# A sliding-window attention layer inside a 17-phase kernel: the attention of the first key heads is issued among the query projections

## The chip, the cores and the metric

The kernel runs on one core of a Trainium2 chip. The metric is device microseconds for one execution, the median of several. Before the change three runs gave 2635.97 us (2631.42 to 2639.07). Engines: PE (TensorE) with its weight loads PEld, DVE (VectorE), ACT (ScalarE), POOL (GpSimd) and SP (SyncE), which here only issues DMAs. The sequence is 256 tokens, the width 1024.

## The reference

Four layers of a mixed network, then a second block. Each layer is feed-forward, mixer, feed-forward, gated projection. The mixer of the third layer (index 2) is the sliding-window attention, and only that one is touched:

```python
def swa_mixer(x, w_qkv, q_gain, k_gain, sinks, w_o):
    q, k, v = jnp.split(x @ w_qkv, [nq, nq + nk], axis=-1)      # 16 query heads, 4 key heads of 64
    q = rmsnorm(q.reshape(B, T, SW_HEADS, SW_HD), q_gain)
    k = rmsnorm(k.reshape(B, T, SW_KV_HEADS, SW_HD), k_gain)
    ...
    s = jnp.einsum('bnqkgd,bnskd->bnkgqs', qb, kk).astype(jnp.float32) * (SW_HD ** -0.5)
    s = s - slopes[:, :, None, None] * dist
    s = jnp.where(valid[None, :, None, None], s, -jnp.inf)      # window of 128 keys
    probs = jax.nn.softmax(jnp.concatenate([s, sink], axis=-1), axis=-1)[..., :-1]
    o = jnp.einsum('bnkgqs,bnskd->bnqkgd', probs.astype(vv.dtype), vv).reshape(B, T, nq)
    return o @ w_o
```

## The kernel before

All weights are cut into units of 128 x 2048 floats (1 MB, 256 output columns over all 1024 inputs). SP loads each unit into one of four raw buffers (L586 in the loop). ACT rounds it to the high part (`high`, L1129), DVE subtracts that from the raw unit to get the low part (`low`, L1535), and PE multiplies high by high, low by high and high by low. Three units have room in split form: `high(m)` waits until unit m-3 has been used, `low(m)` waits for `high(m)`, and PE waits for `low(m)`. Here `n0` is the first unit of the phase, and `low(n0 + u + SPLIT)` prepares the unit three places on.

`project` (L658) runs one unit as 48 matmuls of 256 columns into one PSUM bank; `project_tokens` (L675) does the same with tokens in the rows. Banks 0 to 3 form a ring; DVE empties a bank by `scale` (L1594) or `scale_tokens` (L1600), multiplying by the root of the layer's norm, and counts it in `bank_read`.

The sliding-window phase `sw` has 11 units: in order two of keys, four of queries, one of values, four of the output matrix. Each unit of keys or queries is a pair of 128-feature chunks. Each pair has its own norm per head: ACT squares it (L1412), PE sums the squares by a matmul with a block matrix (`sums`, L1012), ACT takes Ln (L1400) and then Exp (L1406) of the sums, DVE multiplies the pair (`normalise`, L2078). Ln and Exp each come behind a load of the activation table. Before, pairs 0 to 3 do this together and pairs 4 and 5 together.

Then comes the attention, 8 groups: group g is key head g // 2 and query block g % 2, with four query heads. An even group sees 128 keys, an odd one 256. Steps of a group: `scores` (PE, L969), `logits` (DVE: bias L2109, maximum L2036, small sinks L2040 to L2042), `exps` (ACT, L1371 and L1375), `probs` (DVE, L2050 to L2054), `turn` (PE transposes, L979), `copies` (ACT, L1390), `values` (PE, L989), `take` (DVE, L2060). All score banks are double (banks 0 to 3), and so are the value banks (6 and 7); `scores(g + 2)` is issued ahead of `turn(g)`, and `values(g - 1)` behind it. Last, ACT and DVE split the result into two parts (L1423, L2116) and the four output units run (`w_out`), the first of them waiting for each part as it needs it.

Each engine runs its own program in strict order; the order is written out by hand in the function `sw` of each engine, and semaphores join them.

Of the kernel before, what the change touches and what calls it, by code (L numbers as in the profile page):

```python
# [14 lines left out]
P = 128  # L15
# [72 lines left out]
def weight_units(inputs, phases):  # L88
# [3 lines left out]
    for kind, layer in phases:  # L92
# [29 lines left out]
        elif kind == "sw":  # L122
            w = a["sw_w_qkv"][0]
            for u in range(2):
                k0 = SW_HEADS * HD + 2 * u * HD
                yield columns_unit(w, np.concatenate([span(k0, HD), span(k0, HD), span(k0 + HD, HD), span(k0 + HD, HD)]))
# [172 lines left out]
def build(nc, phases, x_t, p_t, mem_t, weights, smalls_d, post_rows, c_common, c_levels, c_swa, c_second, out):  # L299
    begin = starts(phases)  # L300
    NU = begin[-1]["units"]
    with ExitStack() as ctx:
# [173 lines left out]
        def sw_pair(u):  # L476

            c = 8 + 2 * u if u < 2 else 2 * (u - 2)
            return SW_QK[:, c:c + 2]

# [155 lines left out]
        def _(pe):  # L636
# [318 lines left out]
            def attention(g0, groups, bufs, read="exp", late=False):  # L955
# [4 lines left out]
                def scores(g):  # L960
                    if g >= len(groups):
                        return
                    if g >= 2:
                        pe.wait_ge(att[read], g0 + g - 1)
# [18 lines left out]
                def values(g):  # L983
                    pe.wait_ge(att["pt"], g0 + g + 1)
                    if g >= 2:
                        pe.wait_ge(att["taken"], g0 + g - 1)
                    for r, col, vs in groups[g]["values"]:
                        for j, (v, block_) in enumerate(vs):
                            last = nc.tensor.matmul(ps[r, 6 + g % 2, col:col + P], v,  # L989
                                                    PT[g % 2][:, block_ * P:(block_ + 1) * P],  # L990
                                                    start=(j == 0), stop=(j == len(vs) - 1))
# [12 lines left out]
                values(len(groups) - 1)  # L1004

            def sw(i):
# [114 lines left out]
        def _(act):  # L1121
# [237 lines left out]
            def attention(g0, groups, bufs, sinks=False, from_psum=False):  # L1359
                PR, PT = bufs  # L1360

                def exps(g):
                    if g == len(groups):
                        return
# [3 lines left out]
                    if from_psum and g >= len(PR):  # L1368
                        act.wait_ge(att["turned"], g0 + g - len(PR) + 1)
                    if sinks:  # L1370
                        nc.scalar.activation(t[:, 12:16], t[:, 12:16], ACT.Exp, scale=G["scale"])  # L1371
                    for s in range(G["slots"]):
                        p = PR[g % len(PR)][:, s * G["width"] + G["k0"]:(s + 1) * G["width"]]
                        src = ps[:, 2 * (g % 2) + s // 2, (s % 2) * 256:(s % 2 + 1) * 256] if from_psum else p
                        last = nc.scalar.activation(p, src, ACT.Exp, bias=t[:, 4 + s:5 + s], scale=G["scale"],  # L1375
# [3 lines left out]
                exps(0)  # L1379
                for g, G in enumerate(groups):  # L1380
                    exps(g + 1)
# [8 lines left out]
                    nc.scalar.copy(dst, src).then_inc(att["pt"], 1)  # L1390

            def sw(i):
# [3 lines left out]

                def roots(p0, p1):
                    for p in range(p0, p1):
                        act.wait_ge(m["sums"], p + 1)
                        ins = nc.scalar.activation(  # L1400
                            SW_SQ[:, 2 * (p % 4):2 * (p % 4) + 2].rearrange("p c t -> p (c t)"), ps[:, 4 + p % 4, :],
                            ACT.Ln, bias=EPSB, scale=1.0 / HD)
                    link(ins)
                    for p in range(p0, p1):
                        r = SW_SQ[:, 2 * (p % 4):2 * (p % 4) + 2]
# [915 lines left out]
```

## Time and profile before

| what | value |
|---|---|
| median of three runs | 2635.97 us |
| the profiled execution, its own time | 2631.93 us |
| its span | 2630.1 us |
| mean granted clock of TensorE | 0.994 |
| PE busy | 2564.0 us (97%) |
| DVE busy | 1729.3 us (66%) |
| ACT busy | 1203.6 us (46%) |
| mean DMA traffic | 167 GB/s |

The profiled execution took 1.8 us outside its span. All times below are microseconds from the start of the span. Busy time counts an engine as busy while an instruction is in flight, and matmuls overlap each other, so the distance from start to start is the cost of one.

### The profile page before, as it was taken

Reading aid. Unit: us, or ns where it says so; the run is one execution under the profiler, and the core shown is the slowest. Engines: PE = TensorE matmul, PEld = TensorE weight load, DVE = VectorE, ACT = ScalarE, POOL = GpSimd, SP = SyncE. Lnnn points to the kernel's source line nnn. Section 1 sums busy time; section 2 is a strip of 40 time slices with the busy share of each in tenths; the row PEclk is TensorE's granted clock in tenths of the full one; section 3 lists DMA queues with packets and bytes.
Section 4 is the critical chain, followed back from the end, with each engine's and each line's share of the span. In section 5 each row is a group of like instructions: output and inputs, shape, how many; then the busy total and the mean of one; then the engine's idle time right before and its main releaser. Section 6 shows DMA issues by size and latency. Waiting matters only on the chain.

```text
span 2630.1 us, 49686 instructions
## 1 busy us (share of the span) xinstructions
PE 2564.0 (97%) x21160; PEld 2522.5 (96%) x21160; DVE 1729.3 (66%) x2225; ACT 1203.6 (46%) x1277; POOL 29.4 (1%) x62
## 2 busy tenths in 40 slices
PE   8999999999999999999988999999999999999998
PEld 8999999999998999999977999999999999999998
DVE  6557666576566765765576656755866657688664
ACT  4435254444444544453464434534535435444643
POOL 0000000000000000000000000000000000011000
PEclk9999999999999999999999999999999999999999
DMA  6454235544543454454532445544424554445352
GB/s 270 181 187 173 99 134 195 189 176 178 183 170 143 149 192 180 178 184 178 188 134 78 184 176 176 188 181 177 175 97 159 198 177 175 169 133 168 142 188 76
DMA packets 62130, 439.19 MB, mean 167 GB/s; under 512 B 7504, under 2 KB 7632, under 8 KB 9488
## 3 DMA queue, kind: packets, MB, share of 16 engines
q1 hardware_dynamic: 59440, 429.05, 44.8%
q0 software_dynamic: 2528, 7.74, 1.1%
q8 instruction: 131, 2.15, 0.3%
q14 instruction: 31, 0.25, 0.0%
HBM read 432.56 MB, written 1.05 MB: 165 GB/s over the span
## 4 chain that ended last, share of the span: by engine, by line
PE 84%; DVE 10%; ACT 4%; issue 1%; DMA 0%; DVEq 0%; ACTq 0%
PE ps L658 53%; PE ps L689 19%; PE ps L675 6%; DVE w_lo L1535 3%; ACT w_hi L1129 2%; PE ps L804 2%; DVE scratch L1594 1%; DVE x L1653 1%; DVE right_lo L1588 1%; PE ps L927 1%; DVE right_hi L1585 1%; DVE left_lo L1588 1%; PE ps L950 0%; PE ps L936 0%; DVE left_hi L1585 0%
## 5 line engine op out<-in xcount | busy, mean ns | idle before, releaser
L1535 DVE TENSOR_TENSOR w_lo<-raw,w_hi 128x2048 fp32r<-128x2048 f32 x407 | 932.0, 2291 | 500.1 <-ACT w_hi L1129 500.1
L1129 ACT CAST w_hi<-raw 128x2048 fp32r<-128x2048 f32 x407 | 771.6, 1897 | 514.6 <-PE ps L689 249.1
L658 PE MATMUL ps<-right_hi,w_hi 128*128 128x256 f32 x2544 | 727.0, 286 | 7.2 <-DVE right_lo L1588 3.2
L658 PE MATMUL ps<-right_hi,w_lo 128*128 128x256 f32 x2544 | 720.5, 283 | 0.0
L658 PE MATMUL ps<-right_lo,w_hi 128*128 128x256 f32 x2544 | 720.3, 283 | 0.0
L658 PE MATMUL ps<-left_hi,w_hi 128*128 128x256 f32 x1984 | 567.2, 286 | 18.0 <-DVE left_lo L1588 15.2
L658 PE MATMUL ps<-left_hi,w_lo 128*128 128x256 f32 x1984 | 562.1, 283 | 0.0
L658 PE MATMUL ps<-left_lo,w_hi 128*128 128x256 f32 x1984 | 562.1, 283 | 0.0
L658 PEld LDWEIGHTS ps<-right_hi,w_hi 128*128 128x128 f32 x2544 | 488.6, 192 | 13.5 <-issue 5.1
L658 PEld LDWEIGHTS ps<-right_hi,w_lo 128*128 128x128 f32 x2544 | 488.8, 192 | 0.6 <-issue 0.2
L658 PEld LDWEIGHTS ps<-right_lo,w_hi 128*128 128x128 f32 x2544 | 488.8, 192 | 0.0
L658 PEld LDWEIGHTS ps<-left_hi,w_hi 128*128 128x128 f32 x1984 | 381.5, 192 | 21.7 <-issue 14.5
L658 PEld LDWEIGHTS ps<-left_hi,w_lo 128*128 128x128 f32 x1984 | 381.6, 192 | 0.8 <-issue 0.5
L658 PEld LDWEIGHTS ps<-left_lo,w_hi 128*128 128x128 f32 x1984 | 381.5, 192 | 0.0
L1161 ACT ACTIVATE scratch<-scratch 128x256 f32<-128x256 f32 x176 | 73.7, 419 | 583.4 <-DVE scratch L1615 583.3
L689 PE MATMUL ps<-left_hi,w_hi 128*128 128x256 f32 x832 | 236.1, 284 | 2.9 <-DVE right_hi L1585 1.8
L689 PE MATMUL ps<-left_hi,w_lo 128*128 128x256 f32 x832 | 235.4, 283 | 0.0
L689 PE MATMUL ps<-left_lo,w_hi 128*128 128x256 f32 x832 | 235.4, 283 | 0.0
L689 PE MATMUL ps<-right_hi,w_hi 128*128 128x256 f32 x736 | 208.9, 284 | 1.8 <-DVE left_hi L1585 1.8
L689 PE MATMUL ps<-right_hi,w_lo 128*128 128x256 f32 x736 | 208.3, 283 | 0.0
L689 PE MATMUL ps<-right_lo,w_hi 128*128 128x256 f32 x736 | 208.2, 283 | 0.0
L1615 DVE TENSOR_TENSOR scratch<-ps,rstd 128x256 f32<-128x256 f32 x176 | 74.5, 423 | 155.5 <-PE ps L658 126.2
(288 smaller groups left out, 3141.4 us busy)
## 6 DMA issues: line engine op xcount, KB each, us to landing
raw<-weights_dram SPq DMA_DIRECT2D x407, 1024.0 KB, 4.8
scratch<-scratch POOLq DMA_DIRECT2D x48, 64.0 KB, 1.9
x<-x_t_dram SPq DMA_DIRECT2D x1, 1024.0 KB, 6.8
scratch<-c_second_dram POOLq DMA_DIRECT2D x1, 1024.0 KB, 8.8
scratch<-p_t_dram POOLq DMA_DIRECT2D x4, 256.0 KB, 3.0
scratch<-mem_t_dram POOLq DMA_DIRECT2D x1, 1024.0 KB, 6.0
out_dram<-scratch SPq DMA_DIRECT2D x2, 512.0 KB, 3.1
common<-c_common_dram POOLq DMA_DIRECT2D x1, 640.0 KB, 8.9
```

Of the source, the lines that this page charges most:

```text
L658: last = nc.tensor.matmul(bank(e, ring)[:, half * T:(half + 1) * T], l, r, start=(k == 0 and j == 0 and half == 0), stop=(k == KC - 1 and ...
L675: last = nc.tensor.matmul(bank(e, ring)[:, b * T:(b + 1) * T], l, r, start=(k == 0 and j == 0), stop=(k == KC - 1 and j == 2))
L689: last = nc.tensor.matmul(ps[:, 4 + c // 2, (c % 2) * T:(c % 2 + 1) * T], l, r, start=(first and k == 0 and j == 0 and c % 2 == 0), stop=( ...
L804: last = nc.tensor.matmul(o, HG_SUFFIX[:, at_:at_ + keys], upper(HG_PQ[:, at_:at_ + P], w), start=True, stop=True)
L927: last = nc.tensor.matmul(ps[:, 3 + col // 512, col % 512:col % 512 + n], q, k, start=True, stop=True)
L1129: nc.scalar.copy(w_hi[:, m % SPLIT, :], raw[:, m % RAW, :]).then_inc(weights_hi, 1)
L1161: nc.scalar.activation(FFN_T[:, 2 + j % 2], FFN_T[:, j % 2], ACT.Silu).then_inc(silu_ready, 1)
L1535: V.tensor_tensor(w_lo[:, m % SPLIT, :], raw[:, m % RAW, :], w_hi[:, m % SPLIT, :].bitcast(F32), ALU.subtract).then_inc(weights_split, 1)
L1585: V.tensor_scalar(xg_hi[:, c], x[:, c], gain(g, c), None, ALU.mult).then_inc(x_updated, 1)
L1588: V.scalar_tensor_tensor(xg_lo[:, c], x[:, c], gain(g, c), xg_hi[:, c].bitcast(F32), ALU.mult, ALU.subtract).then_inc(xg_ready, 1)
L1594: V.tensor_tensor(dst, pair(e % ring, True), row(rstd[:], 2), ALU.mult).then_inc(bank_read, 1)
L1615: V.tensor_tensor(FFN_T[:, j % 2], pair(e)[:, 0], rstd[:], ALU.mult).then_inc(up_scaled, 1)
```

## The change

Units come in another order: keys of heads 0 and 1, queries of heads 0 to 3, keys of heads 2 and 3, values, then the other three query units. So pairs 0 to 5 are now K01, Q0, K23, Q1, Q2, Q3. The norms of the first three pairs are taken together, each of the other three by itself (`sums(3)`, `sums(4)`, `sums(5)`; `roots(3, 4)` and so on), with the sums' matmuls put inside the passes of the value unit and of query units 5 and 6. The last three query units use only banks 0 and 1, so that banks 2 and 3 are free for scores: there is one buffer for scores now, and one (bank 6) for values. `scores(g)` waits for the `logits` of group g-1. Groups 0 and 1, and the scores of group 2, are issued among the query units. In what is left, PE issues `turn(g)`, `scores(g + 2)`, `values(g)`. The matmuls of `values` alternate between the two halves of the output rows. The splitting of the result is interleaved with groups 4 to 7. On POOL and SP nothing changes but which unit lies where in memory. No arithmetic is added or removed.

```diff
+            yield keys(0)
+            yield columns_unit(w, span(0))
+            yield keys(1)
+            yield columns_unit(w, span((SW_HEADS + SW_KV) * HD))
+            for u in range(1, 4):
                 yield columns_unit(w, span(256 * u))
-            yield columns_unit(w, span((SW_HEADS + SW_KV) * HD))
             for u in range(4):
                 yield columns_unit(a["sw_w_o"][0], span(256 * u))
...
-
-            c = 8 + 2 * u if u < 2 else 2 * (u - 2)
+        SW_UNITS = (0, 1, 2, 4, 5, 6)
+
+        def sw_pair(p):
+
+            c = (8, 0, 10, 2, 4, 6)[p]
             return SW_QK[:, c:c + 2]
+
+        def sw_sums(p):
+            return ps[:, 4 + min(p, 3), :]
+
+        def sw_squares(p):
+            return SW_SQ[:, 2 * (p % 4):2 * (p % 4) + 2]
...
-                    if "ready" in groups[g]:
-                        pe.wait_ge(*groups[g]["ready"])
+                    if g:
+                        pe.wait_ge(att["bias"], g0 + g)
+                    pe.wait_ge(*groups[g]["ready"])
                     for at_, n, q, k in groups[g]["scores"]:
-                        at_ += 1024 * (g % 2)
-                        last = nc.tensor.matmul(ps[:, at_ // 512, at_ % 512:at_ % 512 + n], q, k, start=True, stop=True)
+                        last = nc.tensor.matmul(ps[:, 2 + at_ // 512, at_ % 512:at_ % 512 + n], q, k, start=True, stop=True)
                     last.then_inc(att["scores"], 1)
...
+                    if g:
+                        pe.wait_ge(att["taken"], g0 + g)
+                    heads = groups[g]["values"]
+                    blocks = len(heads[0][2])
+                    for pair_ in (heads[0:2], heads[2:4]):
+                        for j in range(blocks):
+                            for r, col, vs in pair_:
+                                v, block_ = vs[j]
+                                last = nc.tensor.matmul(ps[r, 6, col:col + P], v, PT[g % 2][:, block_ * P:(block_ + 1) * P],
+                                                        start=(j == 0), stop=(j == blocks - 1), skip_group_check=True)
                     last.then_inc(att["out"], 1)
-
-                scores(0)
-                scores(1)
-                for g in range(len(groups)):
-                    if g or not late:
-                        scores(g + 2)
-                    turn(g)
-                    if g == 0 and late:
-                        scores(2)
-                    if g:
-                        values(g - 1)
-                values(len(groups) - 1)
+                return scores, turn, values
...
                 def sums(p):
                     pe.wait_ge(m["sq"], p + 1)
-                    nc.tensor.matmul(ps[:, 4 + p % 4, :], halves,
-                                     SW_SQ[:, 2 * (p % 4):2 * (p % 4) + 2].rearrange("p c t -> p (c t)"),
+                    if p >= 4:
+                        pe.wait_ge(m["rs"], p)
+                    nc.tensor.matmul(sw_sums(p), halves, sw_squares(p).rearrange("p c t -> p (c t)"),
                                      start=True, stop=True).then_inc(m["sums"], 1)
-                mixer_head(i)
-                for p in range(4):
-                    sums(p)
-                project(n0 + 4, e0 + 4, XG)
-                project(n0 + 5, e0 + 5, XG)
-                project_tokens(n0 + 6, e0 + 6, XG)
-                pe.wait_ge(m["rs"], 4)
-                sums(4)
-                sums(5)
-                pe.wait_ge(bank_read, e0 + 7 + 4)
+
+                def first_sums():
+                    for p in range(3):
+                        sums(p)
                 groups = quad_groups(SW_QK, SW_QK[:, 8:12], SW_V, SW_KV, True)
                 for G in groups:
-                    G["ready"] = (m["qk"], 4 if G["kv"] < 2 else 6)
-                attention(att_before(i), groups, ATT_SW, read="bias")
+                    G["ready"] = (m["qk"], (2, 4, 5, 6)[G["kv"]])
+                scores, turn, values = attention(att_before(i), groups, ATT_SW)
+                project(n0, e0, XG, (xg_ready, KC * i))
+                project(n0 + 1, e0 + 1, XG)
+                norm_sums(i)
+                project(n0 + 2, e0 + 2, XG)
+                token_columns(i)
+                project_tokens(n0 + 3, e0 + 3, XG, besides={5: first_sums})
+                project(n0 + 4, e0 + 4, XG, ring=2)
+                pe.wait_ge(bank_read, e0 + 3 + 5)
+                scores(0)
+                project(n0 + 5, e0 + 5, XG, ring=2, besides={2: lambda: sums(3), 5: lambda: scores(1)})
+                turn(0)
+                project(n0 + 6, e0 + 6, XG, ring=2,
+                        besides={1: lambda: sums(4), 3: lambda: scores(2), 6: lambda: values(0)})
+                turn(1)
+                scores(3)
+                sums(5)
+                values(1)
+                for g in range(2, len(groups)):
+                    turn(g)
+                    scores(g + 2)
+                    values(g)
+                pe.wait_ge(bank_read, e0 + 7 + 4)
+                pe.wait_ge(att["bias"], att_before(i) + len(groups))
                 w_out(i, n0 + 7, e0 + 7)
...
-                exps(0)
-                for g, G in enumerate(groups):
-                    exps(g + 1)
+                def copies(g):
+                    G = groups[g]
                     act.wait_ge(att["turned"], g0 + g + 1)
...
+                def square(p):
+                    act.wait_ge(bank_read, e0 + SW_UNITS[p] + 5)
+                    if p >= 4:
+                        act.wait_ge(m["qk"], p - 3)
+                    nc.scalar.activation(sw_squares(p), sw_pair(p), ACT.Square).then_inc(m["sq"], 1)
...
-                for u in range(6):
-                    act.wait_ge(bank_read, e0 + u + 5)
-                    if u >= 4:
-                        act.wait_ge(m["qk"], u - 3)
-                    nc.scalar.activation(SW_SQ[:, 2 * (u % 4):2 * (u % 4) + 2], sw_pair(u),
-                                         ACT.Square).then_inc(m["sq"], 1)
-                    if u:
-                        high(n0 + u + SPLIT)
-                    if u == 3:
-                        roots(0, 4)
-                high(n0 + 6 + SPLIT)
-                roots(4, 6)
-                attention(att_before(i), quad_groups(SW_QK, SW_QK[:, 8:12], SW_V, SW_KV, True), ATT_SW, sinks=True)
-                for u in range(4):
+                def operand(u):
                     act.wait_ge(att["taken"], att_before(i) + 2 * u + 2)
                     nc.scalar.copy(mo_hi[:, 2 * u:2 * u + 2], SW_O[:, 2 * u:2 * u + 2]).then_inc(mo_high, 1)
+                exps, copies = attention(att_before(i), quad_groups(SW_QK, SW_QK[:, 8:12], SW_V, SW_KV, True), ATT_SW)
+                square(0)
+                square(1)
+                high(n0 + 1 + SPLIT)
+                square(2)
+                high(n0 + 2 + SPLIT)
+                roots(0, 3)
+                high(n0 + 3 + SPLIT)
+                square(3)
+                high(n0 + 4 + SPLIT)
+                exps(0)
+                roots(3, 4)
+                exps(1)
+                copies(0)
+                square(4)
+                high(n0 + 5 + SPLIT)
+                roots(4, 5)
+                exps(2)
+                copies(1)
+                square(5)
+                exps(3)
+                roots(5, 6)
+                high(n0 + 6 + SPLIT)
+                for g in range(2, 8):
+                    copies(g)
+                    exps(g + 2)
+                    if g in (4, 6):
+                        operand(g // 2 - 2)
+                operand(2)
+                operand(3)
                 for u in range(4):
...
-                    V.tensor_copy(dst, ps[r, 6 + g % 2, 0:n * P].rearrange("p (c t) -> p c t", t=P)).then_inc(att["taken"], 1)
-
-                logits(0)
-                logits(1)
-                if -1 in besides:
-                    besides[-1]()
-                for g in range(len(groups)):
-                    probs(g)
-                    if g in besides:
-                        besides[g]()
-                    logits(g + 2)
-                    if g:
-                        take(g - 1)
-                take(len(groups) - 1)
+                    V.tensor_copy(dst, ps[r, 6, 0:n * P].rearrange("p (c t) -> p c t", t=P)).then_inc(att["taken"], 1)
+
+                return logits, probs, take
...
-                for u in range(4):
-                    if u == 2:
-                        columns(i)
-                    scale(n0 + u, e0 + u, sw_pair(u))
-                    if u:
-                        low(n0 + u + SPLIT)
-
                 def roots(p):
                     dve.wait_ge(m["rs"], p + 1)
-                    normalise(sw_pair(p), gain(S_SWN, p < 2), SW_SQ[:, 2 * (p % 4):2 * (p % 4) + 2],
-                              m["qk"])
-                for p in range(4):
-                    roots(p)
-                for u in range(4, 6):
-                    scale(n0 + u, e0 + u, sw_pair(u))
-                    low(n0 + u + SPLIT)
-                scale_tokens(n0 + 6, e0 + 6, SW_V, 0)
-                low(n0 + 6 + SPLIT)
+                    normalise(sw_pair(p), gain(S_SWN, int(p in (0, 2))), sw_squares(p), m["qk"])
+
+                def pair_out(p):
+                    scale(n0 + SW_UNITS[p], e0 + SW_UNITS[p], sw_pair(p), ring=BANKS if p < 3 else 2)
...
+                pair_out(0)
+                pair_out(1)
+                low(n0 + 1 + SPLIT)
+                pair_out(2)
+                low(n0 + 2 + SPLIT)
+                columns(i)
+                roots(0)
+                roots(1)
+                scale_tokens(n0 + 3, e0 + 3, SW_V, 0)
+                low(n0 + 3 + SPLIT)
+                roots(2)
+                pair_out(3)
+                logits(0)
+                low(n0 + 4 + SPLIT)
+                logits(1)
+                probs(0)
+                roots(3)
+                pair_out(4)
+                logits(2)
+                probs(1)
+                low(n0 + 5 + SPLIT)
+                take(0)
+                roots(4)
+                pair_out(5)
+                logits(3)
+                probs(2)
+                take(1)
+                low(n0 + 6 + SPLIT)
+                logits(4)
+                roots(5)
+                probs(3)
+                take(2)
+                for g in range(4, 8):
+                    logits(g + 1)
+                    probs(g)
+                    take(g - 1)
+                    if g >= 6:
+                        low_part(g - 6)
+                take(7)
+                low_part(2)
+                low_part(3)
                 residual(i, n0 + 7, e0 + 7)
 
             def second(i):

```

## Rows read from the trace of the kernel before

**Rows 1.** By stretch: length, busy us of PE, PEld, DVE, ACT, POOL; clock, DMA, GB/s.
```profile
1313.20:1366.20 53.00, 49.38 (x366) 44.91 (x368) 33.85 (x44) 33.46 (x33) 0.54 (x1) 0.99 0.41 145
1366.20:1408.60 42.40, 24.95 (x200) 17.76 (x197) 35.48 (x127) 26.38 (x87) 0.00 (x0) 0.82 0.11 44
...
1408.60:1414.60 6.00, 5.99 (x37) 6.00 (x38) 1.67 (x3) 0.00 (x0) 0.00 (x0) 0.72 0.01 3
```

**Rows 2.** The chain that ended last: start, us, what.
```profile
395.49 11.52 PE ps L658 x96
...
1408.61 36.27 PE ps L658 x288
```

**Rows 3.** Timeline of PE: start, us, what, idle before it and its releaser.
```profile
1360.60 1.88 PE L1012 MATMUL ps<-scratch,common 128*128 128x512 f32 x4
...
1374.68 1.12 PE L979 MATMUL ps<-common,scratch 128*128 128x128 f32 x4 [5.10 <-DVE scratch L2054]
1375.73 2.08 PE L969 MATMUL ps<-scratch 64*128 64x256 f32 x8
...
1383.45 1.14 PE L989 MATMUL ps<-scratch 128*64 128x128 f32 x16
1384.52 1.13 PE L969 MATMUL ps<-scratch 64*128 64x256 f32 x8
1386.63 1.09 PE L979 MATMUL ps<-common,scratch 128*128 128x128 f32 x8 [0.98 <-DVE scratch L2054]
1387.65 0.66 PE L989 MATMUL ps<-scratch 128*64 128x128 f32 x8
1388.24 0.72 PE L969 MATMUL ps<-scratch 64*128 64x128 f32 x8
```

**Rows 4.** Timeline of DVE in groups 3 to 6.
```profile
1382.72 0.88 DVE L2109 SCALAR_TENSOR_TENSOR scratch<-scratch,ps 128x128 f32<-128x128 f32 x4
...
1385.04 0.15 DVE L2050 TENSOR_TENSOR tiny<-tiny 128x4 f32<-128x4 f32 x1
...
1386.49 1.41 DVE L2109 SCALAR_TENSOR_TENSOR scratch<-scratch,ps 128x256 f32<-128x256 f32 x4
...
1389.53 0.42 DVE L2060 COPY scratch<-ps 128x256 f32<-128x256 f32 x1
1389.87 0.15 DVE L2050 TENSOR_TENSOR tiny<-tiny 128x4 f32<-128x4 f32 x1
...
1391.06 0.88 DVE L2109 SCALAR_TENSOR_TENSOR scratch<-scratch,ps 128x128 f32<-128x128 f32 x4
```

**Rows 5.** Groups of instructions, 1319 to 1445: shapes, count, busy, mean ns, idle.
```profile
L1535 DVE TENSOR_TENSOR w_lo<-raw,w_hi 128x2048 fp32r<-128x2048 f32 x13 | 29.7, 2288 | 13.5 <-ACT w_hi L1129 13.5
L1129 ACT CAST w_hi<-raw 128x2048 fp32r<-128x2048 f32 x12 | 22.7, 1898 | 21.5 <-PE ps L658 21.5
...
L1594 DVE TENSOR_TENSOR scratch<-ps,rstd 128x512 f32<-128x512 f32 x6 | 4.0, 686 | 3.1 <-ACT rstd L1146 3.1
...
L1400 ACT ACTIVATE scratch<-ps,eps 128x512 f32<-128x512 f32 x6 | 3.7, 689 | 0.0
```

**Rows 6.** Timeline of ACT: norms of four pairs, exponentials of group 1, a copy.
```profile
1344.12 1.28 ACT L1400 ACT_TABLE_LOAD   x1
1345.42 2.43 ACT L1400 ACTIVATE scratch<-ps,eps 128x512 f32<-128x512 f32 x4
1347.86 1.28 ACT L1406 ACT_TABLE_LOAD   x1
...
1371.89 0.20 ACT L1371 ACTIVATE tiny<-tiny 128x4 f32<-128x4 f32 x1 [1.29 <-DVE tiny L2042]
...
1373.87 0.19 ACT L1375 ACTIVATION_READ_ACCUMULATOR scratch<-scratch,tiny 128x1 f32 x1
...
1380.13 1.01 ACT L1390 COPY scratch<-ps 128x1024 f32<-128x1024 f32 x1 [1.74 <-PE ps L979]
```

**Rows 7.** Timeline of DVE: four pairs are normalised, eight instructions.
```profile
1349.82 3.26 DVE L2078 SCALAR_TENSOR_TENSOR scratch<-scratch,smalls 128x256 f32<-128x256 f32 x8 [3.39 <-ACT scratch L1406]
```

More of the change, by code:

```diff
@@ L123, in weight_units, with keys @@
             w = a["sw_w_qkv"][0]
-            for u in range(2):
+            def keys(u):
                 k0 = SW_HEADS * HD + 2 * u * HD
-                yield columns_unit(w, np.concatenate([span(k0, HD), span(k0, HD), span(k0 + HD, HD), span(k0 + HD, HD)]))
-            for u in range(4):
+                return columns_unit(w, np.concatenate([span(k0, HD), span(k0, HD), span(k0 + HD, HD), span(k0 + HD, HD)]))
+            yield keys(0)
[3 more added lines that the diff above has]
+            for u in range(1, 4):
                 yield columns_unit(w, span(256 * u))
-            yield columns_unit(w, span((SW_HEADS + SW_KV) * HD))
             for u in range(4):
@@ L953, in group_steps, with attention @@
                 return scores, turn, values
-            def attention(g0, groups, bufs, read="exp", late=False):
+            def attention(g0, groups, bufs):
                 PR, PT = bufs
@@ L984, in values @@
                     pe.wait_ge(att["pt"], g0 + g + 1)
[L985 to L991, printed above, removed]
-                    last.then_inc(att["out"], 1)
-                scores(0)
-                scores(1)
-                for g in range(len(groups)):
-                    if g or not late:
-                        scores(g + 2)
-                    turn(g)
-                    if g == 0 and late:
-                        scores(2)
-                    if g:
-                        values(g - 1)
-                values(len(groups) - 1)
+                    if g:
[8 more added lines that the diff above has]
+                                                        start=(j == 0), stop=(j == blocks - 1), skip_group_check=True)
+                    last.then_inc(att["out"], 1)
+                return scores, turn, values
             def sw(i):
@@ L1357, in group_steps, with attention @@
                 return exps, copies
-            def attention(g0, groups, bufs, sinks=False, from_psum=False):
+            def attention(g0, groups, bufs):
                 PR, PT = bufs
                 def exps(g):
-                    if g == len(groups):
+                    if g >= len(groups):
                         return
@@ L1367, in exps @@
                     act.wait_ge(att["bias"], g0 + g + 1)
[L1368 to L1371, printed above, removed]
+                    nc.scalar.activation(t[:, 12:16], t[:, 12:16], ACT.Exp, scale=G["scale"])
                     for s in range(G["slots"]):
                         p = PR[g % len(PR)][:, s * G["width"] + G["k0"]:(s + 1) * G["width"]]
-                        src = ps[:, 2 * (g % 2) + s // 2, (s % 2) * 256:(s % 2 + 1) * 256] if from_psum else p
-                        last = nc.scalar.activation(p, src, ACT.Exp, bias=t[:, 4 + s:5 + s], scale=G["scale"],
+                        last = nc.scalar.activation(p, p, ACT.Exp, bias=t[:, 4 + s:5 + s], scale=G["scale"],
                                                     accum_out=t[:, 8 + s:9 + s])
                     last.then_inc(att["exp"], 1)
-                exps(0)
-                for g, G in enumerate(groups):
-                    exps(g + 1)
+                def copies(g):
+                    G = groups[g]
                     act.wait_ge(att["turned"], g0 + g + 1)
@@ L1390, in attention @@
                     nc.scalar.copy(dst, src).then_inc(att["pt"], 1)
+                return exps, copies
             def sw(i):
@@ L1399, in roots @@
                         act.wait_ge(m["sums"], p + 1)
-                        ins = nc.scalar.activation(
-                            SW_SQ[:, 2 * (p % 4):2 * (p % 4) + 2].rearrange("p c t -> p (c t)"), ps[:, 4 + p % 4, :],
-                            ACT.Ln, bias=EPSB, scale=1.0 / HD)
+                        ins = nc.scalar.activation(sw_squares(p).rearrange("p c t -> p (c t)"), sw_sums(p),
+                                                   ACT.Ln, bias=EPSB, scale=1.0 / HD)
                     link(ins)
@@ L2014, in group_steps, with attention @@
                 return logits, probs, take
-            def attention(g0, groups, bufs, out, bias=None, sinks=False, besides={}):
+            def attention(g0, groups, bufs, out, bias=None, sinks=False):
                 PR = bufs[0]
@@ L2110, in alibi, with low_part @@
                     return ins
-                attention(att_before(i), quad_groups(SW_QK, SW_QK[:, 8:12], SW_V, SW_KV, True), ATT_SW,
-                          lambda G: (SW_O[:, 2 * G["kv"]:2 * G["kv"] + 2, G["n"] * P:(G["n"] + 1) * P], slice(0, P), 2),
-                          bias=alibi, sinks=True, besides={-1: lambda: (roots(4), roots(5))})
-                for u in range(4):
+                logits, probs, take = attention(
+                    att_before(i), quad_groups(SW_QK, SW_QK[:, 8:12], SW_V, SW_KV, True), ATT_SW,
+                    lambda G: (SW_O[:, 2 * G["kv"]:2 * G["kv"] + 2, G["n"] * P:(G["n"] + 1) * P], slice(0, P), 2),
+                    bias=alibi, sinks=True)
+                def low_part(u):
                     dve.wait_ge(mo_high, 4 * rcols(i) + u + 1)
```

8 lines of the change are left out of this document (2 added, 6 removed).

## The prediction, written before the changed kernel was run

> **What bounds the kernel now.** The page's busy shares say that PE is in flight nearly all the time, so only stretches in which it is not can give anything. The view by stretch finds the one that the change touches. From 1313.2 to 1366.2, the seven projection units, PE is busy for 49.4 of 53.0 us; from 1366.2 to 1408.6, the attention, for 24.9 of 42.4, while DVE is busy for 35.5, and the granted clock averages 0.82 [rows 1]. The timeline of PE says what it waits for: before a `turn` it waits for `probs` of DVE [rows 3]. The timeline of DVE is what to read next: there every step follows on the last [rows 4]. So DVE paces the attention, and a pair of groups costs it 1.98 + 3.04 (logits) + 1.45 + 1.19 (probs) + 0.68 (takes) = 8.3 us, or 33 of the 48.0 us between the last unit's end at 1360.60 [rows 3] and the start of the output units at 1408.61 [rows 2]. The idle time that could be filled lies earlier: DVE waits 13.5 us for rounded weights among the units [rows 5].
>
> **Prices.** A unit costs PE 5.76 (11.52 for two) [rows 2], a pair's sums 0.86, turn 0.59 (even group) or 1.02 (odd), values 0.59 or 1.07, scores 0.60 or 1.06 (in flight 0.72 and 1.13) [rows 3]. On DVE: logits 1.98 (2.32 less a take of 0.34) or 3.04, probs 1.19 or 1.45 [rows 4], `low` 2.2, `scale` 0.62 (in flight 2.29 and 0.69) [rows 5], a normalised pair 0.81 [rows 7]. On ACT: `high` 1.90, Ln 0.69 [rows 5], table load 1.28, exponentials of an odd group 2.17 (1371.89 to 1374.06), copy 1.01 [rows 6]. The even exponentials, on half the columns, I put at 1.7; 2.17 instead would move only one step below, by 0.4. From engine to engine 0.14 (probs end at 1386.49, turn starts at 1386.63) [rows 3, 4]. I laid the three engines' new orders beside each other and added these up. The same sum over the old order gives 1407.9 at full clock, and 1409.0 with the trace's stretches at the low clock, for the measured 1408.61.
>
> **The change, part by part.** Up to unit 3 nothing differs but what the units are.
>
> *Norms one by one.* Four pairs together cost ACT two table loads; now pairs 3, 4 and 5 bring two each, four more than before: 5.1 us of ACT, 3.9 for each `roots` (two loads, Ln, and an Exp taken like Ln). ACT was busy for 33.5 of 53 us [rows 1], so in itself that is hidden; it costs where someone stands behind it, below.
>
> *Attention inside the units.* Before unit 6 ends PE now also does 3.4 us of groups 0 to 2 and one pair's sums more (0.86). Four waits come in, each with the next matmuls queued behind it. `sums(3)` needs a square, that the scale of unit 4, and this stands on DVE behind `low` and a normalised pair: PE stands 1.6. `turn(0)` needs `probs(0)`, behind `low` and `logits(1)` (3.04): 2.3. `sums(4)` needs a square which ACT does after `exps(1)` and `copies(0)`: 0.9. `sums(5)` needs the scale of unit 6, behind `probs(1)`, `low`, `take(0)` and a pair: 2.1. Unit 6 so ends at 1368.9, 8.3 later than now; `values(1)` at 1375.0, `logits(3)` at 1375.4.
>
> *The last rounding.* `logits(4)` stands on DVE behind `low(n0 + 9)`. Its `high` stands on ACT behind `exps(3)` (1375.5 to 1377.6) and `roots(5, 6)` (3.8), ends at 1383.4, and DVE, done at 1376.9 with `probs(2)` and `take(1)`, is idle for 6.4. `copies(2)`, `values(2)` and so PE's `turn(3)` stand behind the same. `low`, `logits(4)`, a pair and `probs(3)` end at 1389.8. In the old order both last `high` came before the attention.
>
> *One score bank, and scores behind turn.* In the old order the scores of group g+2 are out before `turn(g)`. After the change DVE, having done `probs(g)`, has one take (0.34) left, and `logits(g + 2)` needs turn, then scores. A step is therefore the sum of turn, scores, logits, probs and two handovers: 1.02 + 1.06 + 3.04 + 1.19 + 0.27 = 6.6 from `turn(3)` to `turn(4)`, 0.59 + 0.60 + 1.98 + 1.45 + 0.27 = 4.9 to `turn(5)`, 6.6 to `turn(6)`, against 4.2 in the mean of the old order. To `turn(7)` it is 2.5 (take, a low part, `probs(7)`). From 1389.9 that makes 1410.5. Turn, copy and values of group 7 add 3.1 with handovers.
>
> *The end.* The parts of the first heads lie ready, so `w_out` starts when `values(7)` ends and not a take and a part later (the old order waited 1.2 there); this is in the sum. Start of `w_out`: 1413.8, against 1408.6. The other order of the matmuls in `values`, between row halves, I put at nothing: the bound from above is all of it, 0.07 us a matmul step, from below no loss that a row shows.
>
> *What is hidden.* DVE now waits for the bias table, a DMA of POOL, before its first scale and not before the attention. POOL issues it once x is there, ten us ahead; if it were late, the scales and thus every unit from the fifth would slip with it. SP's loads of two later units leave with the later lows, at about 1371 and 1386; they are needed from about 1425, behind the first output units, and nothing waits.
>
> *The clock.* After an idle 5.1 us scores of an odd group took 2.08 instead of 1.13 [rows 3], and the first 6 us of `w_out` ran at 0.72 [rows 1], so that six units took 36.27 instead of 34.56 [rows 2]: `w_out` is worth 1410.3 in effect. In the new order PE is idle for 6.1, 5.3, 3.3, 2.7 and 3.3 us in turn. If all of the tail runs at 1.2 GHz, turn and scores of groups 3 to 6 and the last turn and values double: 6.7 us more, 1420.5. If none does, 1413.8. Between these I take half, 3.3, by the old order, where the lower level held for part of the attention [rows 1], and 1.7 again for the start of `w_out`: 1418.8, against 1410.3. **Plus 8.5 us.**
>
> What the Trainium skill says of the loads, weighed: here each Ln and Exp has its own load of 1.28, and Ln starts 0.02 behind it [rows 6]. "ScalarE: Activation LUTs", section "Table sets: the hidden batching unit", has Ln and Exp in one set, so that one load would do; by that the sum would lose a part of the 5.1 us of loads, and even with no load at all it ends at 1409.6; the rows differ from the page, and I go by them. Its rule to batch calls by set speaks against this change, and the rows agree.
>
> **The rivals.**
> Clock stays up. For it: in the old attention the clock came back by itself, scores of an odd group at 1384.52 taking 1.13 again [rows 3]. Against: 6.1 and 5.3 us of idle in a row. Plus 3.5 (1413.8 against 1410.3): 2639.5.
> Clock stays down through the tail and into the output units: plus 12 (1420.5 + 1.7 against 1410.3): 2648.
> DVE fills its idle time. In my sum DVE stands idle 16.9 us from its first normalised pair (1343.8) to `probs(7)`: 6.4 for the last rounding, 4.0 for `scores(2)`, 5.1 for scores in the tail, 1.4 in small ones. If DVE's own 50 us were the bound, `w_out` would start at 1396.9, 11.7 earlier: 2623. It decides from 8.5 of those 16.9 on; below that the kernel is slower, and for 0.3% faster all must go. For it speaks that DVE is the bound today [rows 4]; against it the two orders, which put scores behind turn and the rounding behind two table loads. These hold whatever the durations are.
> The overlap does not come about: head start and later stalls cancel, PE's moved work only trades places: 2636.
> A drain behind each load: the page's section "What ACT_TABLE_LOAD costs" gives about 2.7 us for a switch, twice what the rows show. As a mechanism here: each single `roots` would hold ACT 2.8 us longer, and what stands behind it; the four loads that are new would add about 9, 2654. Rows 6 show no gap behind a load.
>
> **How the numbers follow.** The profiled execution took 2631.9; with 8.5 it is 2640.4. It lies 4.0 below the median of the three runs, and the prediction is for a median: 2636.0 + 8.5 = 2644.5. Chances: forecast (plus 6 to 11) 0.50, clock up 0.22, clock down 0.12, no overlap 0.08, DVE's idle filled 0.07, drain 0.01. The range reaches from 2636.5, under the clock-up case with the spread of runs (2631 to 2639), to 2651, over the clock-down case. A measurement of this kernel tells apart about 0.3%, or 7.9 us. Slower by more: 0.7 of the forecast's chance and the two dear cases, 0.35 + 0.12 + 0.01 = 0.48. Within: 0.15 + 0.22 + 0.08 = 0.45. Faster: 0.07. The forecast lies just beyond that bound.
>
> **What would show it.** In the profile after: about ten table loads in the phase; PE waiting before `sums(3)`, `turn(0)` and `sums(4)`; a gap on DVE of about 6 us before the `low` that goes ahead of `logits(4)`, put down to the rounding; then, before each `logits` from group 5 on, 1 to 2 us of DVE waiting for scores; steps of 6.6 and 4.9; the last projection ending some 8 later and `w_out` 5 to 12 later than 1408.6. I am wrong if those gaps are absent, if ACT puts the roots of pair 5 early, or if the clock goes otherwise.

## The result, and the profile after

The changed kernel takes 2645.86 us (2643.59 to 2646.63) where the kernel before takes 2635.54, a ratio of 1.0038 with a 95% interval of 1.0027 to 1.0048: 10 us slower, 7 to 13 (10.3 between the medians). The profiled execution took 2645.3 with a span of 2643.5, that is 13.4 over the one of before. Not all of it belongs to the change. The chain of both kernels has the same pieces in the same order up to the phase, and there the new one is already 1.9 us late, 1.6 of it picked up between 809 and 856 us in a phase that both share. Some experiments below start the phase at 1313, others at 1315, whatever was edited. So a stage is best measured from its own start. From the first matmul of unit 0 to the end of the four output units and the two passes behind them (the row of 288 matmuls) the kernel before takes 1408.61 + 36.27 - 1313.19 = 131.7 us [rows 2]. After the change, the chain has

```profile
1422.13 34.75 PE ps L669 x288
```

and the timeline of PE puts unit 0 at 1315.12, which makes 141.8: 10.1 more.

The timeline of PE in the changed kernel, idle time and its releaser in brackets (L1015 sums, L978 scores, L988 turn, L1002 values):

```profile
1352.83 1.13 PE L1015 MATMUL ps<-scratch,common 128*128 128x512 f32 x2 [0.95 <-ACT scratch L1416]
...
1361.59 0.66 PE L988 MATMUL ps<-common,scratch 128*128 128x128 f32 x4 [2.08 <-DVE scratch L2091]
...
1363.64 2.06 PE L1015 MATMUL ps<-scratch,common 128*128 128x512 f32 x2
...
1375.99 1.12 PE L1015 MATMUL ps<-scratch,common 128*128 128x512 f32 x2 [1.71 <-ACT scratch L1416]
...
1392.85 1.97 PE L988 MATMUL ps<-common,scratch 128*128 128x128 f32 x8 [4.95 <-DVE scratch L2091]
1394.75 1.87 PE L978 MATMUL ps<-scratch 64*128 64x256 f32 x8
```

and of DVE (L1572 is `low`, L2123 the first step of `logits`):

```profile
1367.82 0.88 DVE L2123 SCALAR_TENSOR_TENSOR scratch<-scratch,ps 128x128 f32<-128x128 f32 x4 [4.90 <-PE ps L978]
...
1386.28 2.29 DVE L1572 TENSOR_TENSOR w_lo<-raw,w_hi 128x2048 fp32r<-128x2048 f32 x1 [6.45 <-ACT w_hi L1148]
...
1396.67 1.41 DVE L2123 SCALAR_TENSOR_TENSOR scratch<-scratch,ps 128x256 f32<-128x256 f32 x4 [3.54 <-PE ps L978]
...
1403.37 0.88 DVE L2123 SCALAR_TENSOR_TENSOR scratch<-scratch,ps 128x128 f32<-128x128 f32 x4 [2.05 <-PE ps L978]
...
1410.98 1.42 DVE L2123 SCALAR_TENSOR_TENSOR scratch<-scratch,ps 128x256 f32<-128x256 f32 x4 [3.75 <-PE ps L978]
```

Three new waits are to be seen. DVE stands 4.90 us for `scores(2)`, which PE issues inside unit 6, then 6.45 us for the rounding of the last unit, and from group 5 on each `logits` waits for scores of PE. In the old order DVE went from step to step [rows 4]. Turn and scores at 1392.85 and 1394.75 take 1.97 and 1.87 where the old kernel at full clock took 1.09 and 1.13 [rows 3]. The view by stretch (length, busy us of PE, PEld, DVE, ACT, POOL, then clock, DMA share, GB/s) shows the clock:

```profile
1386.70:1422.00 35.30, 19.83 (x128) 14.60 (x128) 22.01 (x72) 13.50 (x45) 0.00 (x0) 0.62 0.08 30
```

The four added table loads are there too (ten in the phase, six before); the single norm of pair 5 on ACT:

```profile
1380.54 1.28 ACT L1421 ACT_TABLE_LOAD   x1
1381.83 0.69 ACT L1421 ACTIVATE scratch<-ps,eps 128x512 f32<-128x512 f32 x1
1382.54 1.28 ACT L1426 ACT_TABLE_LOAD   x1
1383.83 0.63 ACT L1426 ACTIVATE scratch<-scratch 128x512 f32<-128x512 f32 x1
1384.37 1.88 ACT L1148 CAST w_hi<-raw 128x2048 fp32r<-128x2048 f32 x1
```

The cast in the last row is the rounding for which DVE waits.

### The profile page after: what moved, and what is told of

The parts are those of the page before. It is cut to its first block, busy times and chain, and to the rows that moved or that the text cites. A ratio compares the mean times of both kernels' runs of the same rounds, so it can differ in the third digit from the quotient of the medians.

```text
span 2643.5 us, 49693 instructions
## 1 busy us (share of the span) xinstructions
PE 2570.1 (97%) x21160; PEld 2526.4 (96%) x21160; DVE 1728.7 (65%) x2225; ACT 1208.3 (46%) x1281; POOL 29.3 (1%) x62
## 4 chain that ended last, share of the span: by engine, by line
PE 84%; DVE 10%; ACT 4%; issue 1%; DMA 0%; DVEq 0%; ACTq 0%
PE ps L669 53%; PE ps L700 19%; PE ps L686 5%; DVE w_lo L1572 3%; ACT w_hi L1148 2%; PE ps L815 2%; DVE x L1690 1%; DVE scratch L1631 1%; DVE right_lo L1625 1%; PE ps L938 1%; DVE right_hi L1622 1%; DVE left_lo L1625 1%; PE ps L961 0%; PE ps L947 0%; DVE left_hi L1622 0%
## 5 line engine op out<-in xcount | busy, mean ns | idle before, releaser
L1572 DVE TENSOR_TENSOR w_lo<-raw,w_hi 128x2048 fp32r<-128x2048 f32 x407 | 931.6, 2290 | 500.9 <-ACT w_hi L1148 500.9
```

What stands on the lines that cost most here:

```text
L1572: V.tensor_tensor(w_lo[:, m % SPLIT, :], raw[:, m % RAW, :], w_hi[:, m % SPLIT, :].bitcast(F32), ALU.subtract).then_inc(weights_split, 1)
```

## The experiments

Theory: the loss comes from two places in the hand-written order, the last rounding behind `exps(3)` and `roots(5, 6)` on ACT, and scores behind `turn` on PE; the low clock of an idle PE adds to it. Rivals: it is made inside the units by single norms and stalls; or the lack of a second score bank; or the clock is hidden. All results together, the stage measured as above:

| run | against before | ratio, 95% interval | stage, us |
|---|---|---|---|
| kernel before | | | 131.7 |
| changed kernel | +10.0 us | 1.0038 (1.0027 to 1.0048) | 141.8 |
| e0, changed kernel again | +9.8 us | 1.0037 (1.0023 to 1.0050) | 142.8 |
| e1, early rounding | +4.7 | 1.0018 (1.0009 to 1.0027) | 137.7 |
| e2, two score banks, scores ahead | +3.2 | 1.0012 (1.0003 to 1.0021) | 135.5 |
| e3, both | -4.0 | 0.9985 (0.9976 to 0.9994) | 129.6 |
| e4, PE kept busy | +6.3 | 1.0024 (1.0015 to 1.0033) | 139.1 |
| e5, old order, scores behind turn | +22.4 | 1.0085 (1.0072 to 1.0098) | 152.9 |
| e6, old order, one bank alone | +2.6 | 1.0010 (1.0002 to 1.0019) | 135.1 |
| e8, waits moved in the units | +10.3 | 1.0039 (1.0027 to 1.0051) | 143.1 |
| e9, old order, single norms | +0.3 | 1.0001 (0.9992 to 1.0010) | 132.8 |
| e7, order laid anew | -12.9 | 0.9951 (0.9939 to 0.9963) | 117.2 |

The second column is the distance of the ratio from 1, times the 2635 us of before; the plain differences of the medians lie up to 2 us off it (6.3 for e1, -1.7 for e9). The stage is that of one profiled execution each. e0 repeats the changed kernel on another occasion:

> The changed kernel once more, unchanged, on the same chip and in the same rounds as the run beside it, to have its distance to the kernel before with an interval of its own. Theory and rivals alike: 10 us over the kernel before (8 to 12); where it came out under 8, the distances of the edits to the changed kernel would have to be read as smaller by as much.

It came out 9.8 over before (6 to 13), so the distances below can be read against 10.

**The rounding (e1).**

```diff
+                high(n0 + 6 + SPLIT)
                 square(5)
                 exps(3)
                 roots(5, 6)
-                high(n0 + 6 + SPLIT)
```

> The changed kernel with one line moved on ACT: the rounding of unit n0+9 (high(n0 + 6 + SPLIT)) stands before square(5), exps(3) and roots(5, 6) and not behind them. Theory: the 6.4 us for which DVE stands before the last low, and PE behind it, come from this place in ACT's queue alone; by the sum of durations the output units start 6.0 us earlier than in the changed kernel at either clock, so about 2640 (plus 4 against the kernel before), gap on DVE under 1 us. Rival A, the loss is made inside the projection units by the single norms and their table loads, and the rounding only stands where some other wait would: under 1.5 us gained, 2644.5 or more. Rival B, the loss is the one score bank: the same, under 1.5.

Measured: 5 us gained, 2640.7. In the window from 1368 to 1400 DVE's waits are now

```profile
1384.37 0.88 DVE L2104 SCALAR_TENSOR_TENSOR scratch<-scratch,smalls 128x256 f32<-128x256 f32 x2 [0.47 <-ACT scratch L1426]
1390.79 1.42 DVE L2123 SCALAR_TENSOR_TENSOR scratch<-scratch,ps 128x256 f32<-128x256 f32 x4 [3.75 <-PE ps L978]
1396.83 0.88 DVE L2123 SCALAR_TENSOR_TENSOR scratch<-scratch,ps 128x128 f32<-128x128 f32 x4 [1.38 <-PE ps L978]
```

The 6.45 us gap is gone, the waits for scores stay. One line in ACT's queue made about half of the loss. The output units start 5.6 us earlier in the stage, near the 6.0 of the sum; their first matmuls then ran at the low clock (six passes in 36.29 us, not 34.75), which took 1.5 of it back.

**The scores (e2), and both (e3).**

```diff
+        def score_bank(g):
+            return 0 if g in (4, 6) else 2
...
-                        pe.wait_ge(att["bias"], g0 + g)
+                        pe.wait_ge(att["bias"], g0 + g - (g > 4))
...
-                    src = ps[:, 2:4, :].rearrange("p b t -> p (b t)")[:, 0:n * w]
+                    sb_ = score_bank(g)
+                    src = ps[:, sb_:sb_ + 2, :].rearrange("p b t -> p (b t)")[:, 0:n * w]
...
                 for g in range(2, len(groups)):
-                    turn(g)
                     scores(g + 2)
+                    turn(g)
                     values(g)
```

> The changed kernel with groups 4 and 6 scoring into banks 0 and 1, which are free once the units are scaled, and with scores(g + 2) issued ahead of turn(g) from group 2 on. The rounding stays where the changed kernel has it. Theory: DVE no longer waits for scores in the tail (it waited 3.5, 2.0 and 3.8 us there); by the sum 4.8 us gained at full clock and 6.4 at the low one, about 2640. Rival, ACT and the softmax chain are what paces the tail: under 2 us gained.

> Both edits: the early rounding and two score banks with scores ahead of turn. Theory: the two add up, 10.9 us gained by the sum, so about 2635, level with the kernel before (minus 2 to plus 1 us against it) although all the overlap is kept. Rival, the two gains are the same idle time seen twice: no more than the larger of the two alone, about 2640.

Measured: e2 gains 6.6 of the 9.8 and e3 13.8, where e1 gained 5.1: the two edits add up (11.7) and 2 us more come out, within what the intervals leave. e3 was expected at -2 to +1 us against the kernel before and came out at -4.0; its interval lies wholly below 1, so it beats the kernel before. The waits of DVE for scores of PE have shrunk to 0.68 us in the tail of e3; the longest left is that of the last `take`:

```profile
1386.85 1.42 DVE L2130 SCALAR_TENSOR_TENSOR scratch<-scratch,ps 128x256 f32<-128x256 f32 x4 [0.68 <-PE ps L983]
...
1407.43 0.42 DVE L2104 COPY scratch<-ps 128x256 f32<-128x256 f32 x1 [4.21 <-PE ps L1007]
```

**Which half of the second edit (e5, e6).** The kernel before gets one score bank; in e5 scores also stand behind turn, in e6 they stay ahead.

```diff
-                    if g >= 2:
-                        pe.wait_ge(att[read], g0 + g - 1)
+                    if g:
+                        pe.wait_ge(att["bias"], g0 + g)
...
                 for g in range(len(groups)):
-                    if g or not late:
-                        scores(g + 2)
                     turn(g)
-                    if g == 0 and late:
-                        scores(2)
+                    scores(g + 2)
```

This is e5; in e6 the added `scores(g + 2)` stands ahead of `turn(g)`.

> The kernel before with the tail's ordering of the change and nothing else: one score bank, scores(g) waiting for the logits of group g-1, and scores(g + 2) issued behind turn(g). Units, norms and the start of the attention stay as they were. Theory: scores behind turn puts turn and scores of PE into every step, 7 steps; by the sum 12.4 us slower than the kernel before at full clock, and up to 17 more than that at the low clock, since PE now idles 3 us a step; about 2648. Rival, the step is set by DVE and ACT, PE's part fits beside them: within 2 us of before.

> As the run before, but scores(g + 2) stays ahead of turn(g): the kernel before with one score bank alone. Theory: it is the place of scores behind turn and not the lack of a bank that costs; the sum gives 1.3 us slower than before at full clock, 2 at the low one. Rival, the single bank is the cause: as slow as the run before, 10 us or more.

Measured: 22.4 against 2.6. The lack of a bank alone is not the cause; with one bank, the place of `scores` is. (Two banks with `scores` behind `turn` were not run.) The forecast of about 2648 for e5 missed: 2656 came out. Its 22.4 lie between the 12.4 of the sum at full clock and the 29.4 at the low one, nearer the low one; the mean clock of its steps was 0.64 (1375.0 to 1430.8). Two rows of DVE in e5, one per step, show the mechanism bare:

```profile
1400.76 1.41 DVE L2106 SCALAR_TENSOR_TENSOR scratch<-scratch,ps 128x256 f32<-128x256 f32 x4 [3.47 <-PE ps L969]
1407.79 0.88 DVE L2106 SCALAR_TENSOR_TENSOR scratch<-scratch,ps 128x128 f32<-128x128 f32 x4 [2.37 <-PE ps L969]
```

**The clock (e4).** Behind `values(2)` to `values(5)` stand 6, 5, 4 and 5 extra matmuls into an unused bank.

```diff
+                def keep_busy(n):
+                    pe.wait_ge(m["rs"], 6)
+                    for _ in range(n):
+                        nc.tensor.matmul(ps[:, 7, 0:T], ones, rstd[:], start=True, stop=True)
...
                     values(g)
+                    if g < 6:
+                        keep_busy((0, 0, 6, 5, 4, 5)[g])
```

> The changed kernel with matmuls into the unused bank 7 that nobody reads: 6, 5, 4 and 5 of them behind values(2), values(3), values(4) and values(5), about 0.43 us each at full clock, in gaps of PE of 5, 3.4, 2.6 and 2.5 us. Nothing else is changed; they are extra work. Theory: the low clock costs some 6 us in the tail (turn and scores at double time), so the clock stays at or near its full level from group 4 on and 3 to 5 us are gained, about 2641.5. Rival, the steps of DVE and ACT set the time and the clock of PE is hidden behind them: nothing gained, or up to 3 us lost where the extra matmuls reach past the gap.

Measured: 2641.5, 3.5 us less than the changed kernel over before; the two intervals overlap a little, but the stage is shorter than in both profiles of the changed kernel (139.1 against 141.8 and 142.8). The waits of DVE for scores in the tail fall from 3.5, 2.1 and 3.8 us to 1.9, 1.1 and 1.9. The clock rises as meant, in the stretch that answers to 0.62 above:

```profile
1385.00:1417.40 32.40, 25.73 (x168) 19.16 (x168) 22.45 (x72) 14.89 (x46) 0.00 (x0) 0.84 0.10 33
```

and with it turn(3) and scores(5) are back at full speed, though PE does more:

```profile
1392.66 1.09 PE L988 MATMUL ps<-common,scratch 128*128 128x128 f32 x8
1393.68 1.13 PE L978 MATMUL ps<-scratch 64*128 64x256 f32 x8
```

So the clock was on the path here, because the order had put PE there.

**The units and the norms (e8, e9).** e8 changes only the places inside units 5 and 6:

```diff
-                project(n0 + 5, e0 + 5, XG, ring=2, besides={2: lambda: sums(3), 5: lambda: scores(1)})
-                turn(0)
+                project(n0 + 5, e0 + 5, XG, ring=2, besides={4: lambda: sums(3), 6: lambda: scores(1)})
                 project(n0 + 6, e0 + 6, XG, ring=2,
-                        besides={1: lambda: sums(4), 3: lambda: scores(2), 6: lambda: values(0)})
+                        besides={3: lambda: (turn(0), sums(4)), 4: lambda: scores(2), 7: lambda: values(0)})
```

e9 only splits the norms of the kernel before, on ACT:

```diff
-                        roots(0, 4)
+                        roots(0, 3)
+                        roots(3, 4)
                 high(n0 + 6 + SPLIT)
-                roots(4, 6)
+                roots(4, 5)
+                roots(5, 6)
```

> The changed kernel with PE's waiting steps put later inside units 5 and 6, where what they wait for is nearer: sums(3) at the middle of unit 5, scores(1) at three quarters, turn(0) and sums(4) at three eighths of unit 6. PE's idle time before sums(3), turn(0) and sums(4), 0.95 + 2.08 + 0.13 us in the changed kernel plus what stands inside, shrinks or moves. Theory: these waits are not on the path, since DVE and ACT set when probs(0) and the square of pair 4 come; by the sum 0.7 us gained, 2644. Rival A of the first runs in its other form, the stalls inside the units are lost time like any: 3 us or more gained.

> The kernel before with its norms split as in the change and nothing else: roots(0, 4) becomes roots(0, 3) and roots(3, 4), roots(4, 6) becomes roots(4, 5) and roots(5, 6). That brings four table loads more, 5.1 us of ACT. Theory: most of it is hidden behind the passes of PE; by the sum 1.9 us slower than the kernel before (the loads of the last pair hold up the first exponentials), about 2636.5. Rival, every load of ACT shows: 5 us slower. Second rival, from the Trainium skill, page ScalarE: Activation LUTs: a switch costs 2.7 us with its drain; the four would then be 10.7 us of ACT.

Measured: e8 10.3 over before, the changed kernel 9.8; no gain of 3 us, and whether the 0.7 is there can't be told. e9 0.3 over before, -2.1 to 2.6: a loss of 5 us is ruled out, the 1.9 of the sum fits as well as nothing does. In e9's profile the output units start 2.6 us later in the stage than in the kernel before, and 1.5 of it comes back, because their first matmuls run at the full clock (34.79 us for the 36.27 of before). So most of the loss is not made by the split norms as such. Two limits stay. In the changed order two of the loads do stand on the path, behind `exps(3)` and ahead of the last rounding; e1 moves the rounding away from them. And e8 moves PE's stalls without freeing DVE, which still stands 4.73 us for `scores(2)`:

```profile
1364.94 0.88 DVE L2122 SCALAR_TENSOR_TENSOR scratch<-scratch,ps 128x128 f32<-128x128 f32 x4 [4.73 <-PE ps L978]
```

That wait is in the changed kernel and in e1 to e4 as well; of the runs in the new order only e7 is without it, and no run takes it away alone, so its price is not measured.

**An order laid anew (e7).** Unit order and early start of the change are kept. PE issues scores one to three groups ahead of `turn`, and the values of groups 0 and 4 to 6 behind the `turn` of the next group; ACT does the last rounding behind `copies(3)`, DVE the last two `low` among groups 6 and 7. From PE's program:

```diff
+                sums(0)
+                sums(1)
+                project_tokens(n0 + 3, e0 + 3, XG, besides={1: lambda: (sums(2),)})
+                project(n0 + 4, e0 + 4, XG, ring=2, besides={4: lambda: (scores(0),)})
+                project(n0 + 5, e0 + 5, XG, ring=2, besides={2: lambda: (scores(1), turn(0), sums(3),)})
+                project(n0 + 6, e0 + 6, XG, ring=2, besides={3: lambda: (scores(2), sums(4),)})
...
+                turn(3)
+                scores(6)
+                scores(7)
+                values(3)
+                turn(4)
+                turn(5)
+                values(4)
```

> A version with the unit order of the change, two score banks from group 4 on, and the order of all three engines laid anew by the same sum of durations: sums(0) to sums(2) ahead of and early in the value unit, logits(0) before the scale of unit 4, turn(0) inside unit 5, both last lows among groups 6 and 7, the last rounding behind copies(3), scores one or two groups ahead throughout, values of group g behind turn(g + 1). Theory: if the order of the queues is all that the change got wrong, the overlap pays: the sum puts the start of the output units at 1394 to 1397 on the clock of the trace of before (1408.6 there), 12 to 14 us under the kernel before, about 2622. Rival, DVE fills up or contends and the gain stops at what the two edits together gave: 2630 to 2633.

Measured: 2621.97, a ratio of 0.9951 (0.9939 to 0.9963), 13 us faster than the kernel before and 23 faster than the changed one. Over its last 45 us before the output units DVE is in flight for 42.1:

```profile
1350.00:1395.20 45.20, 35.45 (x289) 28.18 (x286) 42.10 (x121) 38.54 (x91) 0.00 (x0) 0.89 0.20 71
```

DVE's longest wait in this stretch is 0.5 us. Several things differ at once here, so how much each gives is not told apart.

## Why the prediction held, step by step

The forecast was plus 8.5 us, 2644.5; measured are 10.3 between the medians and 10.1 in the stage.

*DVE paces the old attention.* Right as far as the runs show it: e5 makes DVE wait 2.2 to 4.1 us ahead of each `logits` but the first and loses 22.4 us, and e3 and e7, in which DVE waits less, gain; other things differ in those too.

*Stalls inside the units.* The price given for `turn(0)`, 2.3, was measured at 2.08, that for `sums(3)`, 1.6, at 0.95, that for `sums(4)`, 0.9, at 0.13, that for `sums(5)`, 2.1, at 1.7. Unit 6 still ended later than forecast, at 1372.2 or 1370.2 on the clock of before, for 1368.9 (the terms named for it add up to 9.1, not to the 8.3 given). Most of that is a term that the prediction put at nothing, the clock inside unit 6: behind the 2.08 us of idle before `turn(0)`, `sums(4)` took 2.06 us where `sums(3)` took 1.13, so `scores(2)` came about 1 us late and DVE waited 4.90 for it, not 4.0. `logits(3)` was to end at 1375.4 and ends at 1378.3, 1376.4 when the 1.9 us of late start are taken off. e8 shows that moving the stalls later gains nothing clear; the wait of DVE for `scores(2)` is another matter, it stays in e8, and in the changed kernel the chain that ended last runs through it.

*The last rounding.* 6.4 predicted, 6.45 in the trace, and e1 gives back 5. Right.

*Scores behind turn.* Right as a mechanism (e5, e6). DVE's waits were forecast at 1 to 2 us and came out at 3.54, 2.05 and 3.75. The steps came out at 8.2, 5.9 and 8.4 (the turns of groups 3 to 6 start at 1392.85, 1401.05, 1406.96 and 1415.36) for 6.6, 4.9 and 6.6 at full clock. Turn and scores of odd groups took 1.97 and 1.87 to 2.08 us for the 1.09 and 1.13 at full clock, so most of the excess of 4.4 is the low clock.

*The clock.* This is the mis-sized term. Start of `w_out` was put at 1413.8 at full clock, 3.3 us more by half a low tail, 1.7 for its own first matmuls. It starts at 1422.06, on the clock of before 1420.1, so 6.3 us late instead of 3.3. Of these 1.0 were there before the tail, from unit 6 (`turn(3)` starts at 1390.9 on the clock of before, for 1389.9), and 5.3 came in the tail, most of what a tail all at the low clock was to cost (6.7; its own prices, turn and scores of three steps and the last turn and values doubled, add up to 2.08 + 1.19 + 2.08 + 2.09 = 7.4). The mean clock of the tail was 0.62, not half way between the levels. The first matmuls of `w_out` ran at the full clock and lost 0.2, not 1.7. Together 6.5 for 5.0, and that is the 1.5 us by which the forecast of the stage fell short. That the total came so near is in part luck: a tail dearer by 2.0 and a term of 1.0 that was left out stand against a term that was 1.5 too dear.

*What was hidden.* The bias table, SP's later loads and the alternating matmuls of `values` cost nothing that the trace shows: between 1315 and 1425 no row of DVE waits for POOL or a DMA.

*The loads.* The Trainium skill, "ScalarE: Activation LUTs", section "What ACT_TABLE_LOAD costs", adds a drain of about 1.4 us to each load; the rows above start Ln 0.01 us behind the load, and the load 0.02 us behind the last exponential, so this trace does not agree; four loads more make no difference of the medians clear of noise in e9. The same page of the Trainium skill, section "Table sets: the hidden batching unit", has one load for Ln and Exp together; this holds for neither kernel: each has its own.

*The rivals.* "DVE fills its idle time" was given 1396.9 as the start of the output units and did not come about in this order; in e7's order it did, at 1395.3 in a stage that began 0.3 us earlier than that of the kernel before. "Clock stays down" was right for most of the tail and wrong for the output units.

## What to carry to other kernels

Overlap is given away in the order of the queues: for each step that an engine's program puts ahead of the step on the path, ask when that step's input comes, and put nothing slower in front of it. Here a product for a later group had to be issued ahead of the step that waits for this group; one bank less cost 2.6 us, the wrong place of one line 20 more. And when PE is made to wait in short steps, price every step at both clock levels, those among the long passes too: here the tail came out near the low one.

## What was not expected of the hardware

The clock stayed mostly low through 35 us in which PE was in flight for 19.83 of 35.30 us (mean clock 0.62), while the old attention, in flight for much the same share (24.95 of 42.40), held 0.82 [rows 1]. Matmuls that nobody reads, 2.0 to 4.9 us in each of four gaps, raised it to 0.84, and the stage was 2.7 to 3.7 us shorter, not longer.
